# Late squares on ScalarE, an adaLN product ahead of the last x update, and constant matmuls around the norms, in a two-layer decoder trunk

## The chip, the cores and the metric

The kernel runs on one core of one Trainium2 chip, in one launch. The metric is the device time of an execution in microseconds. Three runs of the kernel before took 2462.27, 2471.68 and 2476.03 us, so the median is 2471.68 us.

## What is computed

A residual stream x of 256 tokens by 2048 features goes through four sub-layers. Each is an RMSNorm with an adaLN shift and scale, a mixer or an FFN, and a gated addition to x:

```python
c_act = jax.nn.silu(c)
for layer in range(DEPTH):                       # DEPTH = 2, two sub-layers each
    shift, scale, gate = jnp.split(c_act @ ada_w[layer, 0] + ada_b[layer, 0], 3, axis=-1)
    hn = rmsnorm(x, norm_g[layer, 0]) * (1.0 + scale[:, None, :]) + shift[:, None, :]
    y = rglru_mlstm_mixer(hn, ...) if layer % 2 == 0 else stick_breaking_mixer(hn, ...)
    x = x + gate[:, None, :] * y
    shift, scale, gate = jnp.split(c_act @ ada_w[layer, 1] + ada_b[layer, 1], 3, axis=-1)
    hn = rmsnorm(x, norm_g[layer, 1]) * (1.0 + scale[:, None, :]) + shift[:, None, :]
    x = x + gate[:, None, :] * swiglu(hn, ffn_w1[layer], ffn_w3[layer], ffn_w2[layer])
return rmsnorm(x, final_g)
```

## The kernel before, in words

x lies transposed in SBUF: 16 tiles (chunks) of 128 features by 256 tokens. Weights stream from HBM in chunks of 128 x 2048 (1 MB). ScalarE rounds a chunk to a reduced-precision high part (two halves, line 415), VectorE subtracts it to get the low part (two halves, line 577), and TensorE multiplies the high part by the high and low activations and the low part by the high activations (lines 911 and 913 for the first two chunks behind a norm, 959 and 961 for the others). Both parts have room for four halves, that is two chunks.

The work is cut into bodies of four chunks, s = 0 to 3; `run_stream` gives every engine the same list of bodies. A body splits ahead: at step s it splits the chunk that TensorE needs two steps later (`split_lead`). So in body n, step 2 splits chunk 0 of body n + 1, and step 3 splits chunk 1 of body n + 1. Projections back to x are the bodies out0 (four, behind the layer 0 mixer), down0 (three groups of four, the last one, short, with 12 instead of 16 contraction tiles), out1 and down1. In them VectorE updates one chunk of x at each step (lines 615 and 617). At step 3, and only there, the update stands ahead of the split (`update_first`).

VectorE also computes the adaLN matrix-vector products, one unit of 128 outputs per instruction (line 585, over 1 MB of adaLN weights in `adaw`, which SyncE loads in line 311), between the steps: four units per body in the first two bodies of out0, two per body in the last two, in down0 up to the second short body, and in out1; none in the last two short bodies or in down1. After the last step `add_to_mod` adds a body's results to `mod` (line 592).

A norm stands behind out0 (norm 1), down0 (norm 2), out1 (norm 3) and down1 (norm 4, the final one); norm 0 is in the prologue. GpSimd squares the chunks of x as they are updated and sums the first 15 of them (lines 375 and 381). TensorE sums over partitions with a column of ones (line 980), in two steps, for the sum and for the 16th square. ScalarE takes a root (line 440; the table of functions is loaded ahead of it, in line 438, behind the weight splits that ScalarE still owes), VectorE inverts it (line 699), TensorE spreads it (line 986), and VectorE and ScalarE make 16 tiles of normed activations (lines 703, 447, 709), each of which TensorE multiplies as soon as it is there (line 911). All engines work through their own instructions strictly in order and wait on semaphores.

## Time and profile before

| What | Value |
|---|---|
| Median of the runs, lowest, highest | 2471.68, 2462.27, 2476.03 us |
| Span of the profiled execution | 2464.7 us (its device time is not listed apart) |
| Median of the runs less that span | 7.0 us |
| TensorE busy | 2278.0 us (92%) |
| VectorE busy | 1887.0 us (77%) |
| ScalarE, GpSimd busy | 1028.9 us (42%), 246.4 us (10%) |
| Mean granted TensorE clock | 0.985 of full |

The span goes from the first to the last instruction. Busy time is a sum over the instructions of an engine. The chain of waits follows the end of the program back from each instruction to what released it, so its shares say what held the end. What stands behind the arrow in a row is what the engine had been waiting for.

### The profile page before, as it was taken

The numbers are of one execution on the slowest core, as the hardware profiler recorded it, in microseconds if no ns is written. First come the engines' busy times: TensorE is split into PE (matmuls) and PEld (weight loads), VectorE is DVE, ScalarE is ACT, GpSimd is POOL, SyncE is SP. The second block draws the span as 40 slices with busy tenths as digits, with TensorE's granted clock in tenths as the row PEclk, the third lists the DMA queues.
The fourth block names the chain that finished last, engine by engine and source line by source line (L and its number), as shares of the span: only waits on it lengthen the run. The fifth ranks groups of instructions, "written<-read, shape, count | busy, mean of one in ns | idle before, by whom it ended". The sixth has DMA issues, their size and how long they took to land.

```text
span 2464.7 us, 36210 instructions
## 1 busy us (share of the span) xinstructions
PE 2278.0 (92%) x12638; PEld 1964.7 (80%) x12638; DVE 1887.0 (77%) x2347; ACT 1028.9 (42%) x1183; POOL 246.4 (10%) x209
## 2 busy tenths in 40 slices
PE   0299998989999999999989999998999999999998
PEld 0277877878888888888778888887888888888887
DVE  7888897988877888788896565678887566665667
ACT  1143466344433443333455445534443333333443
POOL 7100001510000000000240000042000000000014
PEclk9999999999999999999999999999999999999999
DMA  8798765867777777777756656665776555555554
GB/s 350 290 369 322 279 270 228 310 231 285 284 278 269 280 273 280 279 276 280 280 205 273 237 222 233 232 250 215 296 289 239 187 188 183 183 183 185 186 202 155
DMA packets 86186, 619.80 MB, mean 251 GB/s; under 512 B 10216, under 2 KB 10472, under 8 KB 10984
## 3 DMA queue, kind: packets, MB, share of 16 engines
q1 hardware_dynamic: 85248, 617.79, 66.2%
q10 hardware_dynamic: 872, 1.15, 0.1%
q8 instruction: 39, 0.64, 0.1%
q14 instruction: 27, 0.22, 0.0%
HBM read 616.80 MB, written 2.10 MB: 251 GB/s over the span
## 4 chain that ended last, share of the span: by engine, by line
PE 83%; DVE 10%; issue 3%; POOL 2%; ACT 2%; DMA 0%; DVEq 0%; POOLq 0%; ACTq 0%
PE ps L959 48%; PE ps L961 24%; PE ps L934 4%; DVE adaw L585 3%; DVE wlow L577 3%; PE ps L911 2%; POOL work L381 1%; POOL work L375 1%; PE ps L913 1%; DVE raw L585 1%; ACT whigh L415 1%; PE ps L1081 0%; DVE work L843 0%; DVE work L615 0%; DMA adaw<-ada_dram 0%
## 5 line engine op out<-in xcount | busy, mean ns | idle before, releaser
L415 ACT ACTIVATE whigh<-raw 128x1024 fp32r<-128x1024 f32 x784 | 828.4, 1061 | 1196.5 <-PE ps L961 1127.6
L959 PE MATMUL ps<-hn,whigh 128*128 128x512 f32 x3712 | 1307.8, 397 | 5.7 <-DVE wlow L577 5.7
L577 DVE TENSOR_TENSOR wlow<-raw,whigh 128x1024 fp32r<-128x1024 f32 x784 | 973.4, 1260 | 404.1 <-ACT whigh L415 397.9
L961 PE MATMUL ps<-hn,wlow 128*128 128x256 f32 x3712 | 1042.0, 281 | 0.0
L959 PEld LDWEIGHTS ps<-hn,whigh 128*128 128x128 f32 x3712 | 697.7, 188 | 174.1 <-issue 7.7
L961 PEld LDWEIGHTS ps<-hn,wlow 128*128 128x128 f32 x3712 | 702.4, 189 | 0.0
L959 PE MATMUL ps<-mid,whigh 128*128 128x512 f32 x1856 | 656.7, 398 | 15.9 <-DVE wlow L577 8.5
L961 PE MATMUL ps<-mid,wlow 128*128 128x256 f32 x1856 | 520.8, 281 | 0.0
L959 PEld LDWEIGHTS ps<-mid,whigh 128*128 128x128 f32 x1856 | 349.1, 188 | 105.1 <-DVE mid L661 8.9
L585 DVE CUSTOM_DVE_ANT_0 adaw<-adaw,cact 128x2048 f32<-128x2048 f32 x176 | 406.9, 2315 | 5.0 <-DMA adaw<-ada_dram 4.9
L961 PEld LDWEIGHTS ps<-mid,wlow 128*128 128x128 f32 x1856 | 351.1, 189 | 0.0
L367 POOL MEMSET work<- 128x256 f32 x5 | 1.6, 312 | 1789.1 <-DVE x L617 1775.6
L934 PE MATMUL ps<-whigh,hn 128*128 128x512 f32 x384 | 120.5, 392 | 1.8 <-DVE work L640 1.1
L604 DVE TENSOR_REDUCE work<-ps 128x256 f32<-128x512 f32 x176 | 120.5, 684 | 0.0
L375 POOL TENSOR_TENSOR work<-x 128x256 f32 x80 | 108.4, 1355 | 116.9 <-DVE x L617 110.5
L381 POOL TENSOR_TENSOR work<-work 128x256 f32<-128x256 f32 x75 | 113.2, 1509 | 5.9
L615 DVE SCALAR_TENSOR_TENSOR work<-ps,mod,x 128x256 f32<-128x256 f32 x128 | 61.2, 478 | 55.8 <-PE ps L961 55.6
L911 PE MATMUL ps<-hn,whigh 128*128 128x512 f32 x128 | 56.0, 469 | 49.4 <-DVE wlow L577 33.3
L934 PEld LDWEIGHTS ps<-whigh,hn 128*128 128x128 f32 x384 | 72.1, 188 | 18.0 <-DVE wlow L577 2.6
L980 PE MATMUL ps<-ones,work 128*128 128x1 f32 x40 | 7.0, 283 | 77.2 <-POOL work L381 70.8
L911 PEld LDWEIGHTS ps<-hn,whigh 128*128 128x128 f32 x128 | 29.1, 227 | 58.8 <-issue 39.5
L934 PE MATMUL ps<-wlow,hn 128*128 128x512 f32 x192 | 74.7, 389 | 0.0
(193 smaller groups left out, 1056.2 us busy)
## 6 DMA issues: line engine op xcount, KB each, us to landing
raw<-wts_dram SPq DMA_DIRECT2D x392, 1024.0 KB, 4.8
adaw<-ada_dram SPq DMA_DIRECT2D x176, 1024.0 KB, 6.7
raw<-ada_dram SPq DMA_DIRECT2D x16, 1024.0 KB, 5.4
x<-xT_dram SPq DMA_DIRECT2D x1, 2048.0 KB, 13.0
out_dram<-x SPq DMA_DIRECT2D x4, 512.0 KB, 2.6
cact<-c_row_dram SPq DMA_DIRECT2D x1, 1024.0 KB, 4.4
work<-lru_w_dram ACTq DMA_DIRECT2D x1, 1024.0 KB, 6.2
mod<-ada_b_dram SPq DMA_DIRECT2D x1, 96.0 KB, 4.0
```

The lines of the kernel that those rows point to most:

```text
L375: pool.tensor_tensor(square, xm, xm, ALU.mult).then_inc(S["square_step"], 1)
L381: pool.tensor_tensor(squares_sum, squares_sum, square, ALU.add).then_inc(S["square_step"], 1)
L415: act.activation(whigh[:, (2 * s + h) % 4, :], raw[:, s, h * HALF:(h + 1) * HALF], ACT.Copy)\
L577: dve.tensor_tensor(wlow[:, half, :], raw[:, s, h * HALF:(h + 1) * HALF], whigh[:, half, :].bitcast(F32), ALU.subtract).then_inc(S["low_re ...
L585: dve.tensor_tensor_reduce(out=place, in0=place, in1=cact[:, :], scale=1.0, scalar=0.0, op0=ALU.mult, op1=ALU.add, accum_out=dots[:, u:u + ...
L604: dve.tensor_reduce(dst, halves_sum(s), AX.X, ALU.add).then_inc(S["chunks_evicted"], 1)
L615: dve.scalar_tensor_tensor(tmp, ps[:, s, 0:T], gate, xm, ALU.mult, ALU.add).then_inc(S["half_added"], 1)
L911: pe.matmul(ps[:, s, :], whigh[:, half, w], src[:, kk, :, :], start=kk == 0, stop=False, skip_group_check=True)
L913: ins = pe.matmul(ps[:, s, T:2 * T], wlow[:, half, w], src[:, kk, 0, :], start=False, stop=kk == KT - 1, skip_group_check=True)
L934: ins = pe.matmul(ps[:, 2 + j, :], hn[:, kk, a, tok], b[:, half, w], start=first, stop=kk == KT - 1 and a == 1, skip_group_check=True)
L959: pe.matmul(ps[:, s, :], whigh[:, half, w], src[:, kk, :, :], start=kk == 0, stop=False, skip_group_check=True)
L961: ins = pe.matmul(ps[:, s, T:2 * T], wlow[:, half, w], src[:, kk, 0, :], start=False, stop=kk == kts - 1, skip_group_check=True)
```

## The change

There are three edits. For the norms 1 to 4, GpSimd squares and sums the first 14 chunks only, and the squares of the last two are made by ScalarE into two tiles of their own, behind the table load; TensorE then has three waits in place of two. In the bodies of the projections back to x, the unit of step 3 and `add_to_mod` go ahead of the update of chunk 3 (and so ahead of the split that stands behind that update). Around the small matmuls of each of these norms TensorE gets matmuls of a constant tile by itself, whose result in bank 6 nobody reads: five between the last two squares, three behind the sum, and six behind the spreading of the root (not in norm 4).

```diff
+        late_squares = [work[:, 30, :], work[:, 33, :]]
+        LATE = KT - 2
@@ GpSimd, squares(norm)
+                count = KT - 1 if norm == 0 else LATE
+                base = 32 + 29 * (norm - 1) if norm else 0
-                with pool.Fori(0, KT - 1) as m:
+                with pool.Fori(0, count) as m:
                     squared(m)
...
-                squared(KT - 1)
+                if norm == 0:
+                    squared(KT - 1)
@@ ScalarE, norm(i)
                 act.activation(warm[:, :], epsb[:, :], ACT.Sqrt)
+                if i:
+                    for late, dst in enumerate(late_squares):
+
+                        act.wait_ge(S["chunks_evicted"], LAST_UPDATE[i] * CH + LATE + late + 1 + CREDIT)
+                        act.activation(dst, x[:, LATE + late, :], ACT.Square).then_inc(S["late_square"], 1)
                 act.wait_ge(S["variance_ready"], i + 1)
@@ VectorE, body
+                    if update_first and units > 0:
+                        units_of(pair, units, s)
+                        add_to_mod(pair * 2, units)
...
                         update_x(n, s, kind.replace("short", ""), q, i)
                         if update_first and units >= 0:
                             split(*split_lead(n, s))
-                    if kind[:2] != "up":
+                    if kind[:2] != "up" and not update_first:
                         units_of(pair, units, s)
...
-                if units > 0:
+                if units > 0 and kind[:3] not in ("out", "dow"):
                     add_to_mod(pair * 2, units)
@@ TensorE, norm
-                    for last, squares in enumerate((squares_sum, square)):
-                        pe.wait_ge(S["square_step"], 32 * c + 31 + last)
+                    def keep_busy(times):
+                        for _ in range(times if c else 0):
+                            pe.matmul(ps[:, 6, 0:P], ones[:, :], ones[:, :], start=True, stop=True, skip_group_check=True)
+
+                    parts = [squares_sum] + (late_squares if c else [square])
+                    for n, squares in enumerate(parts):
...
+                        else:
+                            pe.wait_ge(S["late_square"], 2 * (c - 1) + n)
                         for j in range(2):
...
+                        if n == 1:
+                            keep_busy(5)
                     ins.then_inc(S["variance_ready"], 1)
+                    keep_busy(3)
...
                     ins.then_inc(S["rstd_spread"], 1)
+                    if c < 4:
+                        keep_busy(6)
```

VectorE's instructions at the end of the first body of out0 (steps 2 and 3), before. `adaw` is a unit's adaLN weights, `wlow` the low part of a weight chunk, `work<-ps,mod,x` and `x<-ps,mod,work` are the update of a chunk of x:

```order
L577 TENSOR_TENSOR wlow<-raw,whigh 128x1024 [waits high_ready] x2
L615 SCALAR_TENSOR_TENSOR work<-ps,mod,x 128x256 [waits mod_added,halves_multiplied]
L617 SCALAR_TENSOR_TENSOR x<-ps,mod,work 128x256 [waits half_added]
L585 ISA adaw,dots<-adaw,cact 128x2048 [waits ada_loaded0]
L585 ISA dots 128x1
L615 SCALAR_TENSOR_TENSOR work<-ps,mod,x 128x256 [waits mod_added,halves_multiplied]
L617 SCALAR_TENSOR_TENSOR x<-ps,mod,work 128x256 [waits half_added]
L577 TENSOR_TENSOR wlow<-raw,whigh 128x1024 [waits high_ready] x2
L585 ISA adaw,dots<-adaw,cact 128x2048 [waits ada_loaded1]
L585 ISA dots 128x1
L592 TENSOR_TENSOR mod<-mod,dots 128x4 [waits unit_done]
```

And the same place of the changed kernel:

```order
L625 SCALAR_TENSOR_TENSOR work<-ps,mod,x 128x256 [waits mod_added,halves_multiplied]
L627 SCALAR_TENSOR_TENSOR x<-ps,mod,work 128x256 [waits half_added]
L595 ISA adaw,dots<-adaw,cact 128x2048 [waits ada_loaded0]
L595 ISA dots 128x1
L595 ISA adaw,dots<-adaw,cact 128x2048 [waits ada_loaded1]
L595 ISA dots 128x1
L602 TENSOR_TENSOR mod<-mod,dots 128x4 [waits unit_done]
L625 SCALAR_TENSOR_TENSOR work<-ps,mod,x 128x256 [waits mod_added,halves_multiplied]
L627 SCALAR_TENSOR_TENSOR x<-ps,mod,work 128x256 [waits half_added]
L587 TENSOR_TENSOR wlow<-raw,whigh 128x1024 [waits high_ready] x2
```

The second unit of the two and the addition to `mod` moved ahead of the update and of the split of the next body's chunk 1. The same holds for every body of the projections that has units.

TensorE's instructions of norm 1 before, between the last body of out0 and the first chunk of the FFN:

```order
L980 MATMUL ps<-ones,work 128x1 [waits square_step]
L980 MATMUL ps<-ones,work 128x1
L980 MATMUL ps<-ones,work 128x1 [waits square_step]
L980 MATMUL ps<-ones,work 128x1
L986 MATMUL ps<-ident,rstd 128x128 [waits rstd_ready]
L986 MATMUL ps<-ident,rstd 128x128
L911 MATMUL ps<-hn,whigh 128x512 [waits hn_ready,low_ready,chunks_evicted]
```

And of the changed kernel, from the first late square on (L1003 is line 980 before, L992 is a constant matmul, L1012 is line 986 before, L924 line 911):

```order
L1003 MATMUL ps<-ones,work 128x1 [waits late_square]
L1003 MATMUL ps<-ones,work 128x1
L992 MATMUL ps<-ones 128x128 x5
L1003 MATMUL ps<-ones,work 128x1 [waits late_square]
L1003 MATMUL ps<-ones,work 128x1
L992 MATMUL ps<-ones 128x128 x3
L1012 MATMUL ps<-ident,rstd 128x128 [waits rstd_ready]
L1012 MATMUL ps<-ident,rstd 128x128
L992 MATMUL ps<-ones 128x128 x6
L924 MATMUL ps<-hn,whigh 128x512 [waits hn_ready,low_ready,chunks_evicted]
```

Two matmuls and a wait for a late square were added, and fourteen constant matmuls, eight of them ahead of the spreading of the root.

ScalarE's instructions of norm 1 in the changed kernel (L450 is line 440 before):

```order
L443 ACT_TABLE_LOAD
L443 ACTIVATE warm<-epsb 128x1 [waits consts_ready]
L448 ACTIVATE work<-x 128x256 [waits chunks_evicted] x2
L450 ACTIVATE rstd<-ps,epsb 128x2 [waits variance_ready]
L457 ACTIVATE hn<-work,mod 128x256 [waits scaled_ready] x16
```

The two squares stand between the table load and the root, and no second table load stands around them.

## Rows read from the trace of the kernel before

**Rows 1.** The page, chain that ended last, by engine (share of the span)

```profile
PE 83%; DVE 10%; issue 3%; POOL 2%; ACT 2%; DMA 0%; DVEq 0%; POOLq 0%; ACTq 0%
```

**Rows 2.** Waits of TensorE, whole span: us in total, times, longest us

```profile
PE ps L959 <- DVE wlow L577: 14.2, 12, 4.5
```

**Rows 3.** Timeline, TensorE at norms 1 to 4: start us, us, [idle before <-releaser]

```profile
502.39 0.61 PE L980 MATMUL ps<-ones,work 128*128 128x1 f32 x4 [0.28 <-POOL work L381]
...
1270.54 0.61 PE L980 MATMUL ps<-ones,work 128*128 128x1 f32 x4 [1.48 <-POOL work L381]
...
1694.37 0.61 PE L980 MATMUL ps<-ones,work 128*128 128x1 f32 x4 [0.28 <-POOL work L381]
...
2453.40 0.61 PE L980 MATMUL ps<-ones,work 128*128 128x1 f32 x4 [1.45 <-POOL work L375]
2454.56 0.71 PE L986 MATMUL ps<-ident,rstd 128*128 128x128 f32 x4 [0.55 <-DVE rstd L699]
```

**Rows 4.** Timeline, VectorE, norm 1

```profile
503.22 2.77 DVE L577 TENSOR_TENSOR wlow<-raw,whigh 128x1024 fp32r<-128x1024 f32 x2
505.91 2.28 DVE L585 CUSTOM_DVE_ANT_0 adaw<-adaw,cact 128x2048 f32<-128x2048 f32 x1
...
508.63 0.16 DVE L699 RECIPROCAL rstd<-rstd 128x2 f32<-128x2 f32 x1
510.10 0.87 DVE L703 SCALAR_TENSOR_TENSOR work<-x,slope,ps 128x256 f32<-128x256 f32 x2 [1.31 <-PE ps L986]
```

**Rows 5.** Timeline, VectorE, norm 3

```profile
1702.16 0.87 DVE L703 SCALAR_TENSOR_TENSOR work<-x,slope,ps 128x256 f32<-128x256 f32 x2 [1.31 <-PE ps L986]
```

**Rows 6.** Chain of waits, norm 2: start us, us, what

```profile
1272.10 1.02 PE ps L980 x4
...
1273.14 0.27 ACT rstd L440
...
1273.66 1.24 PE ps L986 x4
...
1274.92 0.49 DVE work L703
```

**Rows 7.** Timeline, ScalarE, norm 2, behind the table load

```profile
1271.47 0.20 ACT L438 ACTIVATE warm<-epsb 128x1 f32<-128x1 f32 x1
```

**Rows 8.** Line 528, squares on ScalarE: ns min/median/max, starts

```profile
L528 ACT ACTIVATE work<-work x8: 405/406/418, 353.3 to 393.9; 128x256 f32<-128x256 f32 x8
```

**Rows 9.** Timeline, TensorE, 128x128 matmuls in f32 at full clock

```profile
1352.55 0.61 PE L1096 MATMUL ps<-shut,ident 128*128 128x128 f32 x4
1352.99 0.60 PE L1092 MATMUL ps<-work,tri 128*128 128x256 f32 x2
```

**Rows 10.** Chain of waits, second body of out0, step 3

```profile
457.99 2.28 DVE adaw L585
...
462.69 0.50 PE ps L959
```

**Rows 11.** Chain of waits, second short body of down0, step 3

```profile
1237.17 1.76 DVE wlow L577
1238.93 2.62 DVE adaw L585
```

**Rows 12.** Timeline, TensorE, third short body of down0, chunk 2

```profile
1243.36 0.50 PE L959 MATMUL ps<-mid,whigh 128*128 128x512 f32 x1 [1.55 <-DVE wlow L577]
```

**Rows 13.** Timeline, VectorE, first body of out1, step 3

```profile
1630.14 2.89 DVE L577 TENSOR_TENSOR wlow<-raw,whigh 128x1024 fp32r<-128x1024 f32 x2
```

**Rows 14.** Timeline, TensorE, out1: two rows 24 contraction tiles apart

```profile
1626.67 0.39 PE L959 MATMUL ps<-mid,whigh 128*128 128x512 f32 x1
...
1634.99 0.39 PE L959 MATMUL ps<-mid,whigh 128*128 128x512 f32 x1
```

**Rows 15.** Windows, norm 1: busy us (x instructions) by engine, PEclk, DMA share, GB/s

```profile
504.00:508.00 4.00, 0.61 (x4) 0.52 (x4) 4.00 (x3) 0.97 (x3) 0.90 (x1) 0.85 0.20 41
```

**Rows 16.** Line 311, loads of adaLN weights, whole span

```profile
DMA to landing us min/median/max: 4.6/6.7/10.4
```

More of the change, by code:

```diff
@@ L216, in bass_trunk @@
             unit_done mod_added c_ready consts_ready pick_ready
-            square_step variance_ready std_ready rstd_ready rstd_spread slope_ready scaled_ready
+            square_step late_square variance_ready std_ready rstd_ready rstd_spread slope_ready scaled_ready
             hn_high_ready hn_ready final_ready
@@ L373, in squared @@
                         pool.wait_ge(S["chunks_evicted"], m + LAST_UPDATE[norm] * CH + 1 + CREDIT)
-                    pool.wait_ge(S["square_step"], m * 2 + 32 * norm + 1)
+                    pool.wait_ge(S["square_step"], m * 2 + base + 1)
                     pool.tensor_tensor(square, xm, xm, ALU.mult).then_inc(S["square_step"], 1)
-                with pool.Fori(0, KT - 1) as m:
+                with pool.Fori(0, count) as m:
                     squared(m)
-                    pool.wait_ge(S["square_step"], m * 2 + 32 * norm + 2)
+                    pool.wait_ge(S["square_step"], m * 2 + base + 2)
                     pool.tensor_tensor(squares_sum, squares_sum, square, ALU.add).then_inc(S["square_step"], 1)
-                squared(KT - 1)
+                if norm == 0:
+                    squared(KT - 1)
             def between(name, c):
@@ L975, in between @@
                 elif name == "norm":
-                    for last, squares in enumerate((squares_sum, square)):
-                        pe.wait_ge(S["square_step"], 32 * c + 31 + last)
+                    def keep_busy(times):
[3 more added lines that the diff above has]
+                    for n, squares in enumerate(parts):
+                        if c == 0:
+                            pe.wait_ge(S["square_step"], 31 + n)
+                        elif n == 0:
+                            pe.wait_ge(S["square_step"], 32 + 29 * c)
+                        else:
+                            pe.wait_ge(S["late_square"], 2 * (c - 1) + n)
                         for j in range(2):
-                            ins = pe.matmul(ps[:, 7, j:j + 1], squares[:, j * P:j * P + P], ones[:, 0:1], start=last + j == 0,
-                                            stop=last == 1, skip_group_check=True)
+                            ins = pe.matmul(ps[:, 7, j:j + 1], squares[:, j * P:j * P + P], ones[:, 0:1], start=n + j == 0,
+                                            stop=n == len(parts) - 1, skip_group_check=True)
+                        if n == 1:
+                            keep_busy(5)
                     ins.then_inc(S["variance_ready"], 1)
+                    keep_busy(3)
                     pe.wait_ge(S["rstd_ready"], c + 1)
```

## The prediction

> **What bounds the kernel now.** I read the chain of waits first: TensorE carries 83% of the way to the end, VectorE 10% [rows 1]. So the kernel ends when TensorE has done its matmuls plus the stretches in which it stands still, and an edit is worth what it does to these stretches. TensorE's waits come next. The steady loops hardly wait: all twelve waits for a split weight chunk at line 959 make 14.2 us [rows 2]. Then the four norms, each read from P, the end of the last projection matmul. P is 502.11, 1269.06 and 1694.09 in norms 1 to 3 (start of the wait in [rows 3]: 502.39 - 0.28 and so on). The first normed tile is begun at line 703 at 510.10, 1274.92 and 1702.16 [rows 4 to 6], so 7.99, 5.86 and 8.07 us behind P. Nothing TensorE does can start earlier, so this distance is the number that two of the edits work on.
>
> Norms 1 and 3 are not held by the squares. VectorE updates the last chunk, splits (2.77 us), computes a unit from 505.91 for 2.28 us, and only then, at 508.63, inverts the root [rows 4]. Norm 2, whose last bodies have no units, is held by the sum over partitions (1.02), the root (0.27), and the spreading (1.24) [rows 6]. TensorE's clock falls to its lower level of 1.2 GHz in each of these three norms: the granted clock is 0.85 on average over 504 to 508 us, a stretch with only 0.61 us of matmuls [rows 15], and in norm 2 line 980 takes 1.02 where it takes 0.61 at full clock, and line 986 1.24 where it takes 0.71 [rows 6, 3].
>
> **The norms after the change.** GpSimd's sum of 14 is long ready at P. ScalarE is what the late squares wait for: behind P it copies the last weight half and loads a table, and its warm-up ends at 1271.67, P + 2.61 [rows 7, 3]. The first square takes 0.41 [rows 8] and is there at P + 3.02, the second, which overlaps it, at about 3.4 (the update of x is done before that, see below). Now TensorE, at full clock: two matmuls for the first square from 3.07, of which the next may start 0.45 later (0.61 less the last result's tail, my estimate from the same row); five constant matmuls of 0.22 each (four passes in 0.44 us are two such matmuls, [rows 9]), 1.10; two for the second square, 0.61 to the result: 5.23. Root and reciprocal with their handovers add 0.52 (0.27, 0.16 and small gaps), 5.75, by when the three constant ones (0.66) are just over. Spreading 0.71, and line 703 starts at P + 6.5. At half clock throughout, the parts are 0.9, 2.2, 0.9, then 1.3 for the three constants, which now end behind the root, then 1.24: P + 9.65. The five constants thus stand in front of a square that has been ready for a microsecond: they cost 1.1 to 2.2 us of the path in each norm, more than the squares' move saves.
>
> Which clock? TensorE idles from about P + 0.5 to P + 3.07, some 2.5 us, against two gaps of 1.96 and 3.28 before in norm 1. It can fall once, but behind that there is work nearly without a gap, so it should come back sooner. I take P + 7.6, between the ends and nearer to full clock. Against 7.99, 5.86 and 8.07 this is -0.4 in norm 1, -0.5 in norm 3, and +1.75 in norm 2, where no unit stood in the way and the sequence through ScalarE is simply longer: +0.85 in all. Ends: at full clock -1.5, +0.65, -1.55 (-2.4 in all); at half clock +1.65, +3.8, +1.6 (+7.0).
>
> [...]
>
> Norm 4: ScalarE loaded its table long before, so the late square is ready 0.41 us behind the update, where GpSimd's was ready at 2453.35 to start line 980 at 2453.40 [rows 3]. That gains about 0.2, and the five constants (1.1 us, begun when the chunk before last is squared) take it back: 0, ends -0.3 and +0.3. Behind line 703, VectorE and ScalarE make a tile each 0.79 us (two instructions of 0.39, [rows 4]), and TensorE needs 0.69 for it at full clock (two pairs of 0.347, [rows 14]: 8.32 us for 24). So there VectorE holds the pace, the six constants are hidden, and a better clock brings little: I count nothing and keep -0.5 per norm for the range.
>
> **The unit ahead of the update.** In the last body it fits: VectorE idles before the last update, so the unit of 2.28 us delays it by about 1 us only and is gone from behind it. That is in the 6.5 above (VectorE is through its splits at P + 4.7, before the root comes). The unit's weights land 6.7 us behind their issue [rows 16], just when VectorE is free for them.
>
> But the edit stands in every body with units, and it also puts the unit and the addition, 2.28 + about 0.4 = 2.7 us, ahead of the split of the next body's chunk 1. Where VectorE has time, nothing happens: TensorE needs that split a whole chunk later, 16 x 0.347 = 5.55 us. Where VectorE is behind, TensorE waits for it. Three places:
> - out0, two bodies with four units each. VectorE has no gap, and the chain runs through it up to 462.69, where TensorE starts chunk 1 of the third body; the unit of step 3 of the second body came after that (the chain shows the unit of step 2, at 457.99, the split, and then TensorE, [rows 10]). Now it comes before: 462.69 + 2.7 less a little handover. TensorE doesn't wait again before norm 1, so this stays: +2.6 (ends 0 and +2.8). The first body's delay of the same kind is absorbed, since its own unit was in the chain already.
> - The short bodies of down0, with 12 x 0.347 = 4.2 us per chunk. TensorE got chunk 1 of the third body at about 1237.2 (first half split when the second starts, [rows 11]) and was held again at chunk 2 until 1243.36 [rows 12]. Now chunk 1 is there at 1237.2 + 2.7 + about 0.3 = 1240.2 and chunk 2 can start at 1244.4: +1.0. The unit's load, needed 2.7 us earlier, may come late; a landing of 10.4 in place of 6.7 has been seen [rows 16]. I take +1.5 (ends 0 and +2.8).
> - out1, first body. The split that starts at 1630.14 [rows 13] has its first half ready at about 1631.7, and TensorE needs it at 1694.09 - 11 x 5.55 = 1633.05. With 2.7 more it is ready at about 1634.5: +1.5 (ends 0 and +1.9).
>
> In the other bodies of down0 splits and units make 8 x 1.39 + 2 x 2.28 = 15.7 of 22.2 us [rows 4, 14], the updates fit into the rest, and the split has a chunk's 5.55 us to be late in: 0. SyncE's weight load of chunk 1 is issued later by the same 2.7 us, and ScalarE wants it most of a body later: 0.
>
> GpSimd loses four instructions per norm, off the path.
>
> **The sum.** 2.6 + 1.5 + 1.5 + 0.85 = +6.5 us. The profiled span is 2464.7, its own time isn't listed, and the median of the runs stands 7.0 above it: 2464.7 + 6.5 + 7.0 = 2478.2. The low ends give -2.4 - 0.3 - 1.5 = -4.2, so 2467.5; the high ones 2.8 + 2.8 + 1.9 + 7.0 + 0.3 = +14.8, so 2486.5.
>
> **Rivals.**
> A. The clock holds and the splits' slack suffices. TensorE works through each norm at 2.4 GHz and the unit's move costs nothing in the loops: -4.2 us, 2467.5. For it: half of the waits in these loops are short. Against it: the chain of waits has no gap of VectorE in out0.
> B. Slower by over 0.5%: the constants at 1.2 GHz. The clock falls in the gap before the first late square, the five constants take 2.2 us ahead of the second, and the norms end at P + 9.65, together with the loops' full price: +14.8, 2486.5. It decides from a clock of 0.5 over P + 3 to P + 8 in all three norms, which alone makes +7.0.
> C. The change doesn't do what it says: the late squares make a norm no shorter since ScalarE's copy, table and squares come one behind the other, and only the unit's move counts, with the loops free. Then norms 1 and 3 gain 1.5 each, norm 2 loses 0.65 to 1.75: about -1.5, 2470.2.
>
> **Chances.** What a measurement of this kernel can tell from no change is about 0.5%, 12.4 us on 2471.7: 2459.3 to 2484.1. My forecast 0.55, A 0.12, B 0.15, C 0.15, something unseen that makes it faster 0.03. The forecast and A and C lie inside the 0.5% but for the scatter of the medians, some 5 us. So faster 0.06, same 0.78, slower 0.16. The range is 2465 to 2488: both sets of ends, with part of the scatter.
>
> **What would show it.** In the profile after: line 703's successor at P + 7.6 in norms 1 to 3, between 6.5 and 9.65; the first late square at P + 2.6; the five constants between two ready squares; a wait of TensorE of 2 to 4 us for the split in the second and third body of out0 at chunk 1, and about 1.5 more in the first bodies of out1 and the short ones of down0. The granted clock from P to P + 10 tells between the ends. I am wrong if the loops show no new wait of TensorE, or if the norms stay at full clock throughout.

## The result and the profile after

The changed kernel takes 2482.41 us (median of 14 runs), the kernel before 2464.26 us (14 runs beside them). The ratio is 1.0077, with a 95% interval of 1.0061 to 1.0093: slower by some 19 us. The time lies 4.2 us above the forecast of 2478.2 us and inside the range of 2465 to 2488, but that is luck of the base: the forecast was built on 2471.7 us for the kernel before, the median of three runs, and fourteen runs give 2464.3. The change itself was forecast at +6.5 us with ends of -4.2 and +14.8. It costs 18 to 19, three times the sum and beyond the upper end, and the likeliest case said no change that can be measured.

Chain of waits and waits of the changed kernel (us in total, times, longest us):

```profile
PE 81%; DVE 10%; issue 3%; POOL 2%; DMA 2%; ACT 2%; DVEq 0%; SPq 0%; POOLq 0%; ACTq 0%
...
DVE adaw L595 <- DMA adaw<-ada_dram: 26.1, 19, 4.9
PE ps L972 <- DVE wlow L587: 25.5, 14, 4.7
...
PE ps L1003 <- ACT work L448: 8.4, 4, 2.6
```

Line 972 is the projection matmul (959 before), 587 the split, 595 the unit. TensorE's waits for a split went from 14.2 to 25.5 us [rows 2], and something new is on the chain: a DMA, with 2% where it had 0% [rows 1]. VectorE waits 19 times for the unit's weights.

**The loops.** VectorE at the end of out0's first body (start us, us):

```profile
435.63 2.69 DVE L595 CUSTOM_DVE_ANT_0 adaw<-adaw,cact 128x2048 f32<-128x2048 f32 x1
438.26 0.08 DVE L595 DVE_READ_ACCUMULATOR2_ANT dots<- 128x1 f32 x1
438.44 0.49 DVE L602 TENSOR_TENSOR mod<-mod,dots 128x4 f32<-128x4 f32 x1
438.85 0.47 DVE L625 SCALAR_TENSOR_TENSOR work<-ps,mod,x 128x256 f32<-128x256 f32 x1
439.36 0.48 DVE L627 SCALAR_TENSOR_TENSOR x<-ps,mod,work 128x256 f32<-128x256 f32 x1
439.76 1.22 DVE L587 TENSOR_TENSOR wlow<-raw,whigh 128x1024 fp32r<-128x1024 f32 x1
```

This is the last unit of the first body. From 435.63 to 438.85 it and its addition take 3.2 us, and they now stand between TensorE and the split at 439.76 (of the second body's chunk 1). TensorE gets the chunk at 441.12, where it had it at 437.77 before (start us, us, idle before; the first line is the kernel before):

```profile
437.77 0.47 PE L959 MATMUL ps<-mid,whigh 128*128 128x512 f32 x1 [1.36 <-DVE wlow L577]
...
441.12 0.76 PE L972 MATMUL ps<-mid,whigh 128*128 128x512 f32 x1 [4.17 <-DVE wlow L587]
441.68 0.41 PE L974 MATMUL ps<-mid,wlow 128*128 128x256 f32 x1
441.90 0.63 PE L972 MATMUL ps<-mid,whigh 128*128 128x512 f32 x1
```

The pitch of a pair is here 0.64 to 0.78 us in place of 0.347 [rows 14]: the clock fell behind the wait. Two windows around it, and two around the same wait in the third short body (busy us of PE, PEld, DVE, ACT, POOL, PEclk, DMA share, GB/s):

```profile
437.00:441.00 4.00, 0.00 (x0) 0.00 (x0) 3.86 (x7) 1.04 (x1) 2.79 (x2) 0.74 0.65 246
441.20:445.00 3.80, 3.80 (x12) 3.22 (x13) 3.80 (x3) 0.00 (x0) 1.84 (x2) 0.50 0.32 95
1248.00:1250.00 2.00, 0.00 (x0) 0.00 (x0) 1.96 (x3) 0.00 (x0) 0.75 (x1) 0.50 0.00 0
1250.20:1254.00 3.80, 3.80 (x12) 3.23 (x13) 3.80 (x3) 0.00 (x0) 1.97 (x2) 0.50 0.26 67
```

0.50 of 2.4 is 1.2 GHz. And the end of the second short body on SyncE's queue (SPq) and VectorE. Its last unit, at 1244.77, stands ahead of the third body's chunk 1:

```profile
1237.05 0.33 SPq L313 DMA_DIRECT2D adaw<-ada_dram  x1
1237.13 2.28 DVE L595 CUSTOM_DVE_ANT_0 adaw<-adaw,cact 128x2048 f32<-128x2048 f32 x1
...
1244.77 2.65 DVE L595 CUSTOM_DVE_ANT_0 adaw<-adaw,cact 128x2048 f32<-128x2048 f32 x1 [1.21 <-DMA adaw<-ada_dram]
```

The load lands 7.7 us behind its issue, within the 4.6 to 10.4 us of [rows 16]. It is needed earlier than before, and it isn't issued earlier: 16.7 us behind the start of the second short body, where it was 15.1 in the kernel before:

```profile
1228.70 0.33 SPq L311 DMA_DIRECT2D adaw<-ada_dram  x1
```

**The norms.** TensorE in norm 2, where P is 1281.45:

```profile
1281.45 0.50 PE L1003 MATMUL ps<-ones,work 128*128 128x1 f32 x4
1284.58 0.60 PE L1003 MATMUL ps<-ones,work 128*128 128x1 f32 x4 [2.63 <-ACT work L448]
1285.05 2.18 PE L992 MATMUL ps<-ones 128*128 128x128 f32 x10
1287.02 0.85 PE L1003 MATMUL ps<-ones,work 128*128 128x1 f32 x4
1287.73 1.42 PE L992 MATMUL ps<-ones 128*128 128x128 f32 x6
1288.99 0.61 PE L1012 MATMUL ps<-ident,rstd 128*128 128x128 f32 x4
```

Line 992 is the constant matmuls, 1003 the sums (980 before), 1012 the spreading (986 before). The first normed tile is begun at line 716 (703 before) at 1289.64. In norm 3, P is 1713.75, and VectorE shows what holds the second late square:

```profile
1714.90 2.29 DVE L595 CUSTOM_DVE_ANT_0 adaw<-adaw,cact 128x2048 f32<-128x2048 f32 x1 [2.22 <-DMA adaw<-ada_dram]
1717.12 0.08 DVE L595 DVE_READ_ACCUMULATOR2_ANT dots<- 128x1 f32 x1
1717.34 0.16 DVE L602 TENSOR_TENSOR mod<-mod,dots 128x2 f32 x1
1717.74 0.48 DVE L625 SCALAR_TENSOR_TENSOR work<-ps,mod,x 128x256 f32<-128x256 f32 x1 [0.25 <-DVE mod L602]
1718.26 0.48 DVE L627 SCALAR_TENSOR_TENSOR x<-ps,mod,work 128x256 f32 x1
```

**A ledger.** I read each stage's length from TensorE's timeline: in a loop from the start of its first ordinary chunk to P, in a norm from P to the first ordinary projection matmul (line 959 before) behind it. For all kernels alike P is here 0.12 us behind the start of the last projection matmul. Out0 counts from the first body's chunk 2, short from the first of the four short bodies, out1 from the first body's chunk 2. "Sum" is the difference to the kernel before. In the two kernels marked *, it holds 1.07 for norm 4, from 3.10 to 4.17 us between P and the spreading; elsewhere norm 4 changed by 0.3 at most, which is left out. The last column is the timed ratio with its interval, over 2465 us. Each row of stages is one execution.

| kernel | out0 | short | out1 | norm 1 | norm 2 | norm 3 | sum | timed |
|---|---|---|---|---|---|---|---|---|
| before | 84.7 | 76.6 | 77.7 | 23.4 | 21.3 | 23.3 | | |
| changed | 89.6 | 82.6 | 82.9 | 24.5 | 23.3 | 24.0 | +19.9 | +19 (15 to 23) |
| unit_only | 89.1 | 81.2 | 80.5 | 25.3 | 21.4 | 22.9 | +13.4 | +10 (5 to 16) |
| late_only | 84.7 | 76.1 | 77.7 | 23.3 | 22.1 | 23.1 | -0.1 | -7 (-12 to -2) |
| late_const | 84.6 | 77.3 | 77.7 | 23.1 | 23.3 | 24.3 | +3.3 | +1 (-4 to +6) |
| unit_late | 88.9 | 80.6 | 79.7 | 22.4 | 21.9 | 23.2 | +9.8 | +10 (5 to 15) |
| load_ahead | 88.4 | 80.1 | 80.3 | 23.3 | 24.6 | 23.3 | +13.0 | +8 (3 to 13) |
| hold_clock | 90.9 | 79.2 | 83.2 | 22.7 | 24.6 | 23.3 | +17.0 | +20 (14 to 27) |
| wait_const * | 85.3 | 75.2 | 77.7 | 22.3 | 20.6 | 22.4 | -2.5 | -1 (-5 to +3) |
| last_unit * | 85.2 | 76.0 | 77.7 | 20.6 | 20.6 | 20.8 | -5.2 | -3 (-7 to 0) |
| best | 84.5 | 75.2 | 77.7 | 20.6 | 20.6 | 20.8 | -7.6 | -6 (-9 to -2) |
| unit_ahead | 88.4 | 79.0 | 80.3 | 21.4 | 21.4 | 22.2 | +5.8 | +7 (3 to 11) |
| warm_ahead | 85.2 | 76.6 | 77.7 | 21.0 | 20.0 | 21.3 | -5.2 | -10 (-15 to -5) |

For the changed kernel the ledger gives 16.2 us in the loops and 3.7 in the norms, together what the times show. How far one execution can be trusted shows in kernels whose loops are the same code. With the unit moved and its load late the three loops take 255.1 us (changed), 250.7 (unit_only) and 249.3 (unit_late); with the load early 248.8 (load_ahead) and 247.7 (unit_ahead). One source of this scatter can be seen. In the first short body TensorE waits 2.7 us in every kernel. Behind it the granted clock fell to 0.50 in nine of the thirteen profiles, the kernel before and the changed one among them, and not in unit_only, unit_late, wait_const and best. That alone makes their short stage 1.4 to 2.8 us shorter. The profiled spans differ by less, 2479.1 - 2464.7 = 14.4. The rest is the pace of matmuls between norm 3 and norm 4, where of the change only GpSimd's squares for norm 4 run: that stretch took 734.2 us before and 728.2 after. At the same granted clock, 200 us show (PE busy us, matmuls, PEclk, DMA share, GB/s), before and then after:

```profile
1950.00:2050.00 100.00, 100.00 (x568) 1.00 0.53 188
2150.00:2250.00 100.00, 100.00 (x568) 1.00 0.52 188
```

```profile
1950.00:2050.00 100.00, 100.00 (x578) 1.00 0.50 189
2150.00:2250.00 100.00, 100.00 (x579) 1.00 0.51 189
```

Over the thirteen profiles this stretch takes 727 to 737 us, in no order that follows the edits, so a span alone can't be compared to a few us here.

### The profile page after: what moved, and what is told of

The parts are those of the page before. It is cut to its first block, busy times and chain, and to the rows that moved or that the text cites. A ratio compares the mean times of both kernels' runs of the same rounds, so it can differ in the third digit from the quotient of the medians.

```text
span 2479.1 us, 36410 instructions
## 1 busy us (share of the span) xinstructions
PE 2292.9 (92%) x12754; PEld 1980.3 (80%) x12754; DVE 1891.4 (76%) x2347; ACT 1031.5 (42%) x1191; POOL 227.1 (9%) x197
## 3 DMA queue, kind: packets, MB, share of 16 engines
q10 hardware_dynamic: 872, 1.15, 0.1%
## 4 chain that ended last, share of the span: by engine, by line
PE 81%; DVE 10%; issue 3%; POOL 2%; DMA 2%; ACT 2%; DVEq 0%; SPq 0%; POOLq 0%; ACTq 0%
PE ps L972 47%; PE ps L974 24%; PE ps L947 4%; DVE adaw L595 3%; DVE wlow L587 2%; DMA adaw<-ada_dram 2%; POOL work L385 1%; DVE work L716 1%; ACT whigh L420 1%; POOL work L379 1%; DVE hn L722 1%; DVE raw L595 1%; PE ps L924 1%; PE ps L1109 0%; PE ps L992 0%
## 5 line engine op out<-in xcount | busy, mean ns | idle before, releaser
L972 PEld LDWEIGHTS ps<-hn,whigh 128*128 128x128 f32 x3712 | 697.6, 188 | 176.7 <-issue 10.8
L972 PE MATMUL ps<-mid,whigh 128*128 128x512 f32 x1856 | 660.7, 401 | 24.6 <-DVE wlow L587 17.3
L972 PEld LDWEIGHTS ps<-mid,whigh 128*128 128x128 f32 x1856 | 352.5, 190 | 113.1 <-DVE wlow L587 13.4
L595 DVE CUSTOM_DVE_ANT_0 adaw<-adaw,cact 128x2048 f32<-128x2048 f32 x176 | 405.8, 2309 | 26.4 <-DMA adaw<-ada_dram 26.1
L379 POOL TENSOR_TENSOR work<-x 128x256 f32 x72 | 98.0, 1361 | 133.8 <-DVE x L627 129.0
L385 POOL TENSOR_TENSOR work<-work 128x256 f32<-128x256 f32 x71 | 101.4, 1428 | 5.6
L924 PE MATMUL ps<-hn,whigh 128*128 128x512 f32 x128 | 52.5, 449 | 44.7 <-DVE wlow L587 33.3
L1003 PE MATMUL ps<-ones,work 128*128 128x1 f32 x56 | 9.7, 282 | 78.0 <-POOL work L385 69.6
L1003 PEld LDWEIGHTS ps<-ones,work 128*128 128x128 f32 x56 | 9.6, 248 | 78.6 <-POOL work L385 69.6
```

Source lines behind the costliest of these rows:

```text
L379: pool.tensor_tensor(square, xm, xm, ALU.mult).then_inc(S["square_step"], 1)
L385: pool.tensor_tensor(squares_sum, squares_sum, square, ALU.add).then_inc(S["square_step"], 1)
L595: dve.tensor_tensor_reduce(out=place, in0=place, in1=cact[:, :], scale=1.0, scalar=0.0, op0=ALU.mult, op1=ALU.add, accum_out=dots[:, u:u + ...
L924: pe.matmul(ps[:, s, :], whigh[:, half, w], src[:, kk, :, :], start=kk == 0, stop=False, skip_group_check=True)
L972: pe.matmul(ps[:, s, :], whigh[:, half, w], src[:, kk, :, :], start=kk == 0, stop=False, skip_group_check=True)
```

## Experiments

**unit_only**: the kernel before with the unit's move alone.

```diff
+                    if update_first and units > 0:
+                        units_of(pair, units, s)
+                        add_to_mod(pair * 2, units)
                     dve.wait_ge(S["halves_multiplied"], n * 8 + 2 * s + 2 + CREDIT)
```

> The kernel before with one part of the change alone: in the bodies of out0, down0 and out1 that have units, the last unit and the addition to mod stand ahead of the last update of x. Squares and norms as before. Theory 1 (the unit's place carries the cost): the loops cost what they cost in the changed kernel, +5.0 us in out0, +5.8 in the short bodies of down0, +5.1 in out1, and the norms change by -0.5 to +0.5: +16 us, ratio 1.006 to 1.007, nearly the whole of the change's 1.008. Rival (the norms carry it; the loops' shifts are an accident of one execution): -3 to +3 us, 0.999 to 1.001. In the profile by theory 1: waits of TensorE for line 577's split of 3 to 4 us at the second body of out0, the second short body and the first body of out1, a granted clock of 0.5 behind each, and over 20 us of VectorE waiting for the DMA of adaw.

Measured: ratio 1.0042 (1.0019 to 1.0064), loops +11.8, norms +1.6; VectorE waits 23.1 us for adaw, 17 times. The rival falls: the unit's place alone makes it slower. But it is half to two thirds of the change's loss, not nearly all as expected: out1 cost 2.9 us here and 5.3 in the changed kernel. And norm 1 became longer by 1.9: where the unit waits for its weights, the last update, GpSimd's square and all behind it wait too.

**late_only**: late squares, no constant matmuls, the unit where it was (the change without its edits in `body` and without `keep_busy`).

> The kernel before with the last two squares of norms 1 to 4 by ScalarE and three sums on TensorE, but no constant matmuls and the unit where it was. Theory 1: norms 1 and 3 are held by the unit (line 703 at P + 8.0, as before), norm 2 by warm-up, two squares, the sum, the root and the spreading: 3.42 + 1.0 + 0.3 + 0.2 + 1.24 = P + 6.2 against 5.86, so 0 to +0.5 us, ratio 1.000. Rival (the late squares alone make a norm longer, since ScalarE's table load stands ahead of them): norm 2 at P + 8 and norms 1 and 3 at over P + 9, together over +4 us, 1.002.

Measured: 0.9973 (0.9952 to 0.9993), norms -0.1, +0.7, -0.2. TensorE in norm 2 (P 1269.31):

```profile
1269.31 0.50 PE L1000 MATMUL ps<-ones,work 128*128 128x1 f32 x4
1272.44 1.76 PE L1000 MATMUL ps<-ones,work 128*128 128x1 f32 x8 [2.63 <-ACT work L448]
1274.75 1.22 PE L1009 MATMUL ps<-ident,rstd 128*128 128x128 f32 x4 [0.55 <-DVE rstd L709]
```

As expected by the stages; the rival falls. The time came out better than expected: the interval of -12 to -2 us leaves out the ledger's -0.1 and the expected ratio of 1.000. No stage explains it. I hold it for scatter of the pace, and that isn't shown.

**late_const**: the changed kernel with the unit back behind the update.

> The changed kernel with the unit put back behind the last update: late squares and constant matmuls, loops as before. Theory 1: the loops' 15.9 us are gone; norm 2 keeps P + 8.2 (+2.3 us), norms 1 and 3 stand at P + 7.9 to 8.5 (0 to +0.5 each), and the six constants behind the spreading hold the first projection matmul up by up to 0.6 where the clock is low: +2.5 to +4 us, ratio 1.001 to 1.0016. Rival (the constants are what costs): +8 us or more, 1.003 and up. Rival (the constants pay by the clock): below 1.000.

Measured: 1.0005 (0.9985 to 1.0026), norms -0.3, +1.9, +1.0, ledger +3.3: as expected. Against late_only, norm 2 shows the five constants as 1.66 us of delay of the last sum (P + 4.53 to P + 6.19).

**unit_late**: the changed kernel without constants (`for _ in range(0)` in `keep_busy`).

> The changed kernel without its constant matmuls (late squares and the unit's new place stay). Theory 1: loops +15.9, norm 1 at P + 7.4, norm 2 at P + 6.2, norm 3 at P + 8.1, since there the last update comes 4 to 5 us behind P: +15.5 to +16.5 us, ratio 1.0063 to 1.0067, a little better than the changed kernel's 1.0077 (by 4 us of constants in the norms). Rival (the constants pay by keeping the clock up): slower than the changed kernel, 1.008 or more, with a granted clock of 0.5 for 10 us in each norm in place of 3.4 to 6.8.

Measured: 1.0041 (1.0022 to 1.0061). The size is +10 in place of +16, since the loops cost 10.4 here. That the change's constants pay is refuted: without them the norms are 4.2 us shorter than in the changed kernel (2.1, 1.4 and 0.8). That is more than the 3.7 us that the changed kernel lost in its norms. The loops hold no constants, so the rest of the difference between the two kernels isn't theirs.

**load_ahead**: the changed kernel with SyncE's order turned.

```diff
                 for s in range(CH):
+                    for u in range(s * units // CH, (s + 1) * units // CH):
+                        sp.wait_ge(S["unit_done"], pair * 2 + u + 1)
+                        sp.dma_start(adaw[:, u % 2, :], ...)
                     if units >= 0:
                         sp.wait_ge(S["low_ready"], n * 8 + 2 * s + 2)
                         sp.dma_start(raw[:, s, :], ...)
-                    for u in range(s * units // CH, (s + 1) * units // CH):
...
```

> The changed kernel, with one difference on SyncE's queue: in each step the unit's weights are loaded ahead of the chunk's weights and not behind them, so the last unit's load no longer waits until chunk 3 of the same body is split. Theory 1 (VectorE waits 26 us for adaw because the load stands behind that wait on SyncE): VectorE's waits for adaw fall to under 8 us; out0 keeps its first wait (no adaw wait stood ahead of it), its later ones go: total 88.0 in place of 89.6; short bodies 79.8 in place of 82.6; out1 79.6 in place of 82.9; norms 1 and 3 shorter by 0.5 to 1. Together 8 to 9 us less than the changed kernel: ratio 1.0045 (1.003 to 1.0055). Rival (the load itself is slow, since the DMA engines are loaded with the chunks' weights): waits for adaw stay above 20 us, or the chunks' weights come late in its place, ratio 1.007 or more.

Measured: 1.0033 (1.0014 to 1.0051), against 1.0077. VectorE's waits for adaw:

```profile
DVE adaw L595 <- DMA adaw<-ada_dram: 4.9, 1, 4.9
```

Of 19 waits one is left, of the length of the one that the kernel before had. Loops 88.4, 80.1, 80.3: within 0.7 of what I expected. So the weights were late because SyncE issues them behind a chunk's load that waits for the split of chunk 3. That is clear from the waits; what they cost is less so. The changed kernel and this one differ by 6.3 us in the loops, but unit_late, with late loads, took 249.3 there and this kernel 248.8. Out0's first wait stays, as expected (4.4 us ahead of the chunk). Norm 2 took 24.6, 1.3 more than in the changed kernel: its clock was at 0.50 for 6.8 us in place of 3.4.

**unit_ahead**: unit_only with the same turn on SyncE.

> The kernel before with the unit ahead of the update in every body with units, and its load ahead of the chunk's weights on SyncE's queue; norms as before. Theory 1 (two causes in the loops: the order on VectorE costs some 10 us, the late load the rest): no wait for adaw in the loops, totals of 88.4, 80.1 and 80.3 as in the changed kernel with the early load (+10 us against before), norms 1 and 3 shorter by 0.5 to 1 each: +8 to +9 us, ratio 1.0035 (1.002 to 1.005), below the 1.0042 of the unit's move alone. Rival (the late load was the whole cost): 1.000 to 1.001, totals of 85 to 86, 77 and 78.

Measured: 1.0028 (1.0011 to 1.0045); loops +8.9, norms -3.0. The order on VectorE alone thus costs about 9 us in the loops with every weight in time, and the move does shorten norms 1 and 3, by 2.0 and 1.1 us (expected 0.5 to 1 each). The ratio lies within what was expected, but its interval overlaps with unit_only's, so the times alone don't show what the earlier load brings.

**hold_clock**: constants in three of the loops' waits.

```diff
                     pe.wait_ge(S["chunks_evicted"], n * CH + s + 1)
+                    if s == 1 and isinstance(n, int):
+                        for _ in range({OUT0 + 1: 12, IN1 - 2: 12, OUT1 + 1: 6}.get(n, 0)):
+                            pe.matmul(ps[:, 6, 0:P], ones[:, :], ones[:, :], start=True, stop=True, ...)
```

> The changed kernel with constant matmuls in three of the loops' new waits, ahead of the wait for the split of chunk 1: twelve (2.6 us at full clock) in the second body of out0 and in the third of the short ones, six in the second body of out1 (the last two short bodies and the second of out1 are written out instead of looped for it). Theory 1 (behind a wait the clock falls, but where VectorE is what the next chunk waits for, the slower chunk costs nothing): the chunk behind the wait takes 5.6 to 5.7 and 4.2 in place of 7.8, 6.3 and 7.2 us; out0's total stays within 0.5 of 89.6, short falls from 82.6 to 80.5 to 81, out1 from 82.9 to about 81: -2 to -4 us, ratio 1.0065. Rival (the lower clock is a good part of the cost everywhere): out0 falls by 2 us too and the ratio to 1.005. Rival (constants don't keep the clock): chunks as slow as before, and the totals up by what the constants take.

Measured: 1.0083 (1.0058 to 1.0108), not the 1.0065 expected. TensorE in out0:

```profile
437.77 2.84 PE L965 MATMUL ps<-ones 128*128 128x128 f32 x24
442.11 0.50 PE L977 MATMUL ps<-mid,whigh 128*128 128x512 f32 x1 [1.50 <-DVE wlow L589]
442.57 0.39 PE L977 MATMUL ps<-mid,whigh 128*128 128x512 f32 x1
...
468.14 0.79 PE L977 MATMUL ps<-mid,whigh 128*128 128x512 f32 x1 [3.16 <-DVE wlow L589]
```

The clock held, and the chunk took 5.8 us in place of 7.8. TensorE then waited 3.16 us at the next body's chunk 1 where it had waited 0.96, and began it 49.3 us behind the first ordinary chunk, as in the changed kernel (49.2). So behind out0's first wait the lower clock costs nothing: VectorE sets when the next body's chunk 1 is ready. But the clock fell at that later wait instead (0.50 from 467.2 for 6.8 us), and the chunk there took 8.3 us in place of 5.8. Only a part of that was given back, and out0 ended 1.3 us later than in the changed kernel. In the short bodies it did cost: chunk 1 of the third took 4.3 in place of 6.3, and no wait gave it back (79.2 in place of 82.6, of which another 1.5 is a clock that didn't fall in the second body, where nothing was edited). In out1 the chunk gained 1.6 us. The wait ahead of it grew from 3.0 to 3.8 us, and short later waits and the slower pace of matmuls (chunks of 5.65 us in place of 5.55) took the rest; why the wait grew is open. Theory 1 fell for out1 and for the time.

**wait_const**: late squares, unit behind the update, constants only where TensorE waits.

```diff
-                        if n == 1:
-                            keep_busy(5)
+                        if n == 0:
+                            keep_busy(10)
...
-                    keep_busy(3)
+                    keep_busy(2)
...
-                        keep_busy(6)
+                        keep_busy(4)
```

> The kernel before with the late squares and with constant matmuls only where TensorE waits in a norm: ten behind the first sum (2.2 us of a wait of 2.6), none between the late squares, two behind the variance, four behind the spreading; the unit stays where it was. Theory 1 (the five constants between the two late squares stand on the path; those in a true wait cost nothing and keep the clock at 2.4 GHz): last sum in norm 2 at P + 4.0 to 4.5 in place of 6.2, first ordinary projection matmul at P + 21.0 to 21.5 in norm 2 (23.3 with the change's constants, 22.1 without any, 21.3 before), 22.5 to 23 in norms 1 and 3: 0 to -1.5 us in all, ratio 0.999 to 1.000. Rival (constants don't raise the clock): low clock for 10 us as before, norm 2 at 22.1 or more.

TensorE in norm 2 (P 1268.43):

```profile
1268.79 2.48 PE L989 MATMUL ps<-ones 128*128 128x128 f32 x20
1271.56 1.05 PE L1000 MATMUL ps<-ones,work 128*128 128x1 f32 x8 [0.29 <-ACT work L448]
1272.47 0.69 PE L989 MATMUL ps<-ones 128*128 128x128 f32 x4
1273.17 0.71 PE L1009 MATMUL ps<-ident,rstd 128*128 128x128 f32 x4
```

Norm 2 is 20.6, better than expected, and 2.7 below the change's. The same kind of matmul costs when it stands between two ready squares and pays when it fills the idle time ahead of them: norms 1 to 3 are 3.2 us shorter than in late_only. The granted clock stayed at 1.00 in norms 1 and 2, fell for 3.4 us in norm 3, and in late_only was at 0.50 for 10.2 us in each. The Trainium skill's page "TensorE: Matmul & The Clock Gate", section "What's actually happening", states that "the default state is throttled, and activity releases the throttle". The traces agree, with matmuls of a constant tile as the activity. The time is 0.9996 (0.9978 to 1.0013), which doesn't show the gain: late_only was timed at 0.9973. I had not thought of norm 4, where TensorE doesn't wait and the ten constants cost 1.07.

**last_unit**: in addition, the unit ahead of the update only in the last bodies of out0 and out1 (written out), with its load ahead.

```diff
-                    if update_first and units > 0:
+                    last = update_first and isinstance(n, int) and n in (OUT0 + 3, OUT1 + 3)
+                    if last:
                         units_of(pair, units, s)
                         add_to_mod(pair * 2, units)
```

> As the kernel with constants in the waits only, and the unit ahead of the last update in the last body before norms 1 and 3 alone, where VectorE is idle ahead of that update, with its load issued ahead of the chunk's weights in that body. Theory 1: loops as before (out0 84.7, out1 77.7), no unit behind P in norms 1 and 3, which then end like norm 2: P + 21.5 to 22.3 in place of 23.4; -2 to -4 us in all against before, ratio 0.9985 (0.997 to 1.000). Rival (the unit's place costs in the last body too, by its load): the last update over 2 us behind P, norms 1 and 3 at P + 23.4 or more, ratio 1.000 to 1.002.

Measured: 0.9986 (0.9971 to 1.0001), norms 20.6, 20.6, 20.8. Out0 at 85.2 and out1 at 77.7 are what wait_const had without the unit's move, and in neither norm does a unit stand behind P. The rival falls.

**best**: the same without constants in norm 4 (`times if 0 < c < 4 else 0`).

> The kernel with the unit ahead in the last body before norms 1 and 3 alone (its load ahead too), late squares, constants in true waits; now without constants in norm 4, where TensorE doesn't wait and ten of them stood ahead of two ready squares (spreading at P + 4.2 in place of 3.1). Theory 1: norms 1 to 3 at P + 20.6 to 20.8 for the first ordinary projection matmul, norm 4's spreading at P + 2.9: 6 to 6.5 us less than before, ratio 0.9975 (0.996 to 0.999). Rival (what is gained in the norms is lost by a cost elsewhere, as the ratio 0.9986 of the last version lets one suspect): 0.999 or more.

Measured: 0.9976 (0.9962 to 0.9990), 2457.1 us: faster than both kernels. Of the ledger's -7.6 the norms give 6.2, and 1.3 are the short stage, where the clock didn't fall at a wait that no edit touches. By the times it can't be told from late_only (0.9973), so what the constants and the unit add to the late squares is shown by the lengths of the norms alone. The three norms (busy us of PE, PEld, DVE, ACT, POOL, PEclk):

```profile
503.00:523.00 20.00, 18.55 (x113) 15.04 (x111) 18.17 (x42) 13.05 (x24) 0.00 (x0) 1.00 0.36 144
1265.80:1286.00 20.20, 18.58 (x113) 15.04 (x111) 17.45 (x39) 13.21 (x24) 0.00 (x0) 1.00 0.37 152
1690.00:1710.80 20.80, 18.69 (x114) 15.17 (x113) 18.90 (x42) 13.50 (x25) 0.00 (x0) 1.00 0.36 144
```

**warm_ahead**: ScalarE's warm-up ahead of its last two copies, two constants in the first wait.

```diff
+                    if s == 3 and isinstance(n, int) and n in (OUT0 + 3, IN1 - 1, OUT1 + 3):
+                        act.activation(warm[:, :], epsb[:, :], ACT.Sqrt)
...
-                            keep_busy(10)
+                            keep_busy(2)
```

> As the kernel without constants in norm 4, and ScalarE's table load and warm-up put ahead of its last two copies in the last body before norms 1 to 3, with two constants in the first wait instead of ten (the last two short bodies are written out). Theory 1 (the table load is next on the path in norm 2, VectorE's split in norms 1 and 3, where the unit moved it behind P): norm 2 gains 0.5 to 1 us (P + 19.7 to 20.1), norms 1 and 3 0 to 0.3: ratio 0.0003 below that kernel's, too little to see in the times. Rival (ScalarE loads another table for its copies, so that the load comes twice): norms longer by 1.3.

ScalarE ahead of norm 2:

```profile
1263.22 1.28 ACT L437 ACT_TABLE_LOAD   x1
1264.51 0.20 ACT L437 ACTIVATE warm<-epsb 128x1 f32<-128x1 f32 x1
1265.02 1.06 ACT L431 ACTIVATE whigh<-raw 128x1024 fp32r<-128x1024 f32 x1 [0.30 <-PE ps L989]
```

The table is loaded once, so the rival falls. Norm 2 is 20.0, shorter by 0.5, but norms 1 and 3, expected to be 0 to 0.3 shorter, are longer by 0.4 and 0.5: with two constants in place of ten the clock fell again (3.4 us in norms 1 and 2, 6.8 in norm 3). Its time, 0.9960 (0.9941 to 0.9979), overlaps with that of best, and the ledger (-5.2) doesn't put it ahead; which of the two is faster is open.

## Why the prediction was right and wrong

The time fell into the range, but not for the reasons that the forecast gave. Two of its terms failed, the base (too high) and the loops (too low), and the two errors cancelled in part.

*The base* (the median of the runs, 7.0 us above the span) was 7.4 us too high. In nearly every run that lists both, the time stands 1.7 us above the span (2480.77 and 2479.1 in the changed kernel's profiled execution). The rest was the scatter of three runs, and the kernel before comes to 2464.3 over fourteen. With that base the same sum gives 2470.8 us with ends of 2460 to 2479, and the 2482.4 measured lie outside.

1. *What bounds the kernel*: right. The loss is TensorE's waits at a split and in the norms, as the ledger adds up.
2. *Norms, the sequence on TensorE*: right in norm 2. The first late square reached TensorE at P + 3.13 (forecast 3.07), and the five constants stood in front of a ready square for 1.97 us (1.1 to 2.2). Line 716 begins at P + 8.19, where I took 7.6 of 6.5 to 9.65. What the constants cost is shown by unit_late: 4.2 us in the three norms.
3. *Norms 1 and 3* ("the unit delays the last update by about 1 us only"): wrong. It began at P + 0.5 and P + 1.15, behind waits of 1.25 and 2.22 us for its weights, and the update ended at P + 4.3 and P + 5.0. Line 716 stands at P + 9.44 and P + 8.89. Behind the same P, 0.16 earlier than that of rows 4 to 6, the three norms lost 1.29, 2.17 and 0.66, +4.1 where I had +0.85 (+3.7 to the first ordinary matmul). In norm 3 TensorE waited 0.55 us for the square behind the late update. In norm 1 it didn't wait for it: the constants, at a clock of 0.50 from 510.6, took until 513.54 by themselves.
4. *"The unit's weights land 6.7 us behind their issue, just when VectorE is free for them"*: this step failed. The landing was right (6.6 to 7.7), the issue wasn't: it is bound to the split of chunk 3 on SyncE's queue, and I asked only how long the load takes. load_ahead turned it and left one of 19 waits. Its price is less sure: 1.2 + 2.5 + 2.6 us in the loops of the changed kernel against load_ahead, 3.0 in the loops and 4.6 in the norms of unit_only against unit_ahead, and 0.5 in the loops of unit_late against load_ahead.
5. *The price of the order in the loops* (2.6 + 1.5 + 1.5, ends 0 and 2.8, 2.8, 1.9): the mechanism was right and the size wrong, beyond all three upper ends: 4.9, 6.0 and 5.3. With the weights in time it is 3.8, 2.5 and 2.6 (unit_ahead). In out0 I took the first body's delay for absorbed. It wasn't: the second body's chunk 1 starts 23.4 us behind the first ordinary chunk where it was 20.5, and the third's 49.2 where it was 45.4, so most of the delay there is already the first body's. The unit and its addition took 3.2 us at the first of these places, where I counted 2.7. The rest of what the terms lack isn't taken apart. This term failed by most: 5.6 us were forecast for the loops, they cost 16.2, and the order alone costs 9 to 10 with the weights in time (unit_ahead 8.9, load_ahead 9.9).
6. *The clock in the loops*: not in the forecast at all. It fell to 1.2 GHz behind the new waits (438.9, 1227.4, 1247.9 and 1650.6 us). hold_clock shows that this costs nothing behind out0's first wait, where the next wait takes it up, and 2.0 us in the third short body.
7. *The clock in the norms*: right. It fell once and came back sooner: 6.8, 3.4 and 6.8 us where each had 10.2. What that gives back is less than what the constants take (unit_late).
8. *Full down0 bodies 0, norm 4 0*: right. From the wait in the first down0 chunk of group 0 (698.5 us before, 705.1 after) to that of group 1 it is 272.9 us in both, and from norm 4's P to the end 13.25 us before and 13.21 after.
9. *Rivals*: A and C fall, since all three loops show new waits. C's first half holds: late squares alone made no norm shorter by more than 0.2 us (late_only). B had the direction. Its +14.8 us is nearer to the 18 to 19 measured than any other, and too small as well. But B's mechanism, the lower clock from P + 3 to P + 8 in all three norms, isn't what happened: norm 2 had it for 3.4 us, and the loops cost 16.2 where B allowed 7.5. I gave slower 0.16, too little, since each loop's term was capped by about the 2.7 us of the unit itself.

Open: why the loops cost 16.2 us in the changed kernel's profile and 10.4 and 11.8 in unit_late's and unit_only's, which have the same order there. Where the clock falls accounts for a part: behind the first short body's wait it fell in the changed kernel and not in the other two, which makes 1.6 us. The rest lies mostly in out1, whose wait was 3.0 us against 1.5 and 1.6. One profile of each can't settle it.

## What to carry to other kernels

When an instruction that needs a loaded buffer is moved earlier, follow the load's issue through the queue that issues it, not only its landing time: an in-order queue may hold it behind a wait that has nothing to do with it. Move work ahead of a wait only in the bodies where the engine really has that wait; in a loop where the engine is behind, everything queued behind the moved work is late with it. Filler matmuls belong in idle time that exists, and never between two inputs that are ready.

## What the runs showed of the hardware

- Constant matmuls in a norm's waits kept the granted clock at 1.00 through norms 1 to 3 (last_unit, best), where it had been 0.50 for 10.2 us in each before; with two in place of ten it fell for 3.4 to 6.8 us (warm_ahead).
- In the loops most waits in which TensorE stood idle for 1.9 to 4.9 us were followed by 3.4 to 6.8 us at 0.50, but not all. It stayed at 1.00 behind 3.1 us idle (unit_late, second short body, whose chunk took 4.3 us), behind 2.4 (unit_only, third body of out0), 2.3 (hold_clock) and 2.1 (unit_ahead). The same 2.7 us in the first short body brought it down in nine profiles of thirteen.
- At a granted clock of 1.00 a chunk of 32 matmuls takes 5.55 us or 5.65 us, for hundreds of microseconds at a time and at other places in each execution (568 against 578 matmuls in 100 us). Chunks of 24 take 4.16 or 4.24 us. No row shows what decides it.
- A clock that is held gains nothing where another engine sets the end: 2.0 us won in out0 came back as 2.2 us of wait one body later, and behind that longer wait the clock fell (hold_clock).
- Turning two issues on SyncE's queue took VectorE's waits for the unit's weights from 19 times and 26.1 us to one of 4.9 us (load_ahead).
